# Two RMS norms moved onto scores and a last sum, and cross attention written as a pipeline of heads

## The chip, the cores and the metric

One Trainium2 chip, of which the kernel uses one core. The metric is the device time of one execution in microseconds (us), the median of several runs. The engines of the core are TensorE (PE, matmuls; PEld are its weight loads), VectorE (DVE), ScalarE (ACT), GpSimd (POOL) and SyncE (SP, which here issues the loads of weights). Each engine works through its own queue of instructions in order and waits at semaphores for the others.

## The reference

Two blocks of a language model on 256 tokens of 1024 features, all in float32: a first block (an RWKV mixer, an attention mixer, two gated feed-forward layers, layer norms) and a second one. The change touches the second half of the second block only:

```
def rmsnorm(x, g):
    y = xf * lax.rsqrt(jnp.mean(xf * xf, axis=-1, keepdims=True) + EPS)
    return y * g

def cross_attention(h, memn, w_q, w_kv, w_o):       # 4 heads of 256, 256 memory tokens
    q = (h @ w_q)
    k, v = jnp.split(memn @ w_kv, 2, axis=-1)
    s = jnp.einsum('bqhd,bmhd->bhqm', q, k) * (X_DH ** -0.5)
    p = jax.nn.softmax(s, axis=-1)
    o = jnp.einsum('bhqm,bmhd->bqhd', p, v)
    return o @ w_o

x = x + jnp.concatenate([ml_out, fx_out], axis=-1) @ w_out[l]
x = x + cross_attention(rmsnorm(x, ln_x[l]), rmsnorm(mem, ln_mem[l]), ...)
u = jax.nn.relu(rmsnorm(x, ln2[l]) @ w_ff1[l])
x = x + (u * u) @ w_ff2[l]
return rmsnorm(x, ln_f)
```

The factor of an RMS norm is one number per token. It can be taken out of a product with weights: the scores of a token scale with it, and so does relu, whose square scales with the factor squared.

## The kernel before

Tokens are two tiles of 128 (`t` = 0, 1), features eight tiles of 128 (`k` = 0 to 7). `x_tm` holds the residual with tokens on partitions, `ps` is PSUM with eight banks of 512 columns. A product in near-float32 takes three matmuls (`three`): every operand is split into a high part and the rest (`x_hi`, `x_lo`, `w_hi`, `w_lo`).

Weights come in slabs of 128x2048 in one fixed order: in the part in question `mix_o` (4 slabs), `x_q` (4), `x_o` (4), then `ff2` (32, up and down slabs in turn). SP loads slab i into one of three raw buffers (L531) as soon as `w_lo` of slab i-3 is written. ACT casts it to `w_hi` (`hi`, L575, from `after(i)` as slab i+3, which waits for `slab_done` of slab i), DVE writes `w_lo` (`lo`, L1248). PE waits for `lo_done` of a slab. All these stand at fixed places in the queues of ACT and DVE, between the work on activations. A "wide" slab is 48 matmuls of 256 columns (`wide_fm`), a "tall" slab is four units (`tall_unit`: token tile t, column half n) of six matmuls of 512 columns; a unit that ends a sum signals `bank_done` or `slab_done`.

`last_two(a, b, ...)` runs the last two slabs of a product in the order a(0,0) a(0,1) b(0,0) b(0,1) a(1,0) b(1,0) a(1,1) b(1,1). DVE adds each finished bank to `x_tm` (`add_product`, L1482). An RMS norm (`norm(6)` ahead of x_q, `norm(7)` ahead of ff2, `norm(8)` at the end) is then: ACT squares and sums the rows (L837, L846), takes the root (L838, L848), DVE the reciprocal (L1493), both write `xn` = x_tm * rstd (L1506, L862). PE transposes `xn` (L2289, 8 per token tile). ACT writes `x_hi` = transposed * gain for each k (L870), DVE `x_lo` (L1529). The first wide slab takes k by k as `x_lo` comes (`wide_as_ready`).

Cross attention is written stage by stage: four slabs of x_q with `xq_fm` taken by ACT (L978), the scores of all four heads (L2612), `masked` for all heads (DVE, row maximum, L1665), `exps` (ACT, L986), `probs` (DVE, L1678), transposes (L2362), `take_pt` (ACT, L993), outputs (L2621), `take_o` (ACT, two copies, L1001 and L1002; the next head's waits for `out_low` of this one) and `out_low` (DVE, L1683). `product("x_o", 12)` starts when all four heads are taken.

Of the kernel before, what the change touches and what calls it, by code (L numbers as in the profile page):

```python
# [13 lines left out]
P = 128  # L14
# [147 lines left out]
def build(nc, d, out, upto=99):  # L162
# [4 lines left out]
    with ExitStack() as ctx:  # L167
# [268 lines left out]
        rstd_ready, xn0_ready, xn_act, xn_dve = sem("rstd_ready"), sem("xn0_ready"), sem("xn_act"), sem("xn_dve")  # L436
        mem_loaded, final_ready = sem("mem_loaded"), sem("final_ready")
# [8 lines left out]
        STATS_BEFORE = {0: 0, 1: 2, 2: 4, 3: 6, 4: 8, 6: 11, 7: 14, 8: 17}  # L446
# [117 lines left out]
        def _(act):  # L564
# [330 lines left out]

            def norm(q, second=None):
# [7 lines left out]
                else:  # L904
# [4 lines left out]
                    if q == 8:  # L909
                        return  # L910
                    normalized(q, 1, x_tm)
# [232 lines left out]
            for i in range(2):  # L1144
                after(first["x_o"] + i)
            norm(7)
            for i in (2, 3):
                after(first["x_o"] + i)
            ffn("ff2")
# [86 lines left out]
        def _(dve):  # L1236
# [238 lines left out]
            def add_product(src, scale, t, n, last_slab, product, base=0):  # L1475
# [5 lines left out]
                at = src[:, t, 512 * n:512 * n + 512]  # L1481
                return V.scalar_tensor_tensor(at, at, scale, ps[:, base + 2 * t + n, :], ALU.mult, ALU.add)  # L1482
# [69 lines left out]
            def norm(q, scale, last_slab, product):  # L1552

                base = 0 if q else 2
                if NORMS[q][4]:
                    first_half_sums(scale, last_slab, product, base)
                    scales(q, 0)
                    link(add_product(x_tm, scale, 1, 1, last_slab, product, base))
                    link(half_statistics(1, 1))
                    mean_variance(1)  # L1560
                else:
                    add_product(x_tm, scale, 0, 0, last_slab, product)
                    add_product(x_tm, scale, 0, 1, last_slab, product).then_inc(stat_ready, 1)
                    add_product(x_tm, scale, 1, 0, last_slab, product).then_inc(stat_ready, 1)
                    scales(q, 0)
                    normalized(q, 0, slice(0, C), x_tm)
                    add_product(x_tm, scale, 1, 1, last_slab, product).then_inc(stat_ready, 1)
# [92 lines left out]
            def masked(u, s, tiles, mask):  # L1660
# [9 lines left out]
                V.tensor_scalar(mx[:, n:n + 2], rs[:, n:n + 2], -1.0, None, ALU.mult).then_inc(masked_ready, 1)  # L1670
# [218 lines left out]
            norm(6, 1.0, first["mix_o"] + 3, 5)  # L1889
            for i in (2, 3):  # L1890
                after(first["mix_o"] + i)
            for j in range(4):
                after(first["x_q"] + j)
            link(V.memset(zero_m[:, :], 0.0))
            for u in range(4):
                masked(U_X + u, cr_s, FULL, lambda w, t, c0, c1: zero_m[:, :])
            for u in range(4):
                probs(U_X + u, cr_s, FULL)
            for u in range(4):
                out_low(O_X + u, cr_o, slice(2 * u, 2 * u + 2))  # L1900
            for i in range(2):
                after(first["x_o"] + i)
            norm(7, 1.0, first["x_o"] + 3, 6)
            for i in (2, 3):
                after(first["x_o"] + i)
            ffn("ff2")
            last_norm(first["ff2"] + 31, 7)
# [3 lines left out]
        def _(pe):  # L1911
# [18 lines left out]
            def wide_as_ready(i, hi_x, lo_x, bank, order, x_ready):  # L1930
# [3 lines left out]
                for n, (k, count) in enumerate(order):  # L1934
                    pe.wait_ge(x_ready, count)
# [743 lines left out]
```

## Time and profile before

| | |
|---|---|
| runs | 1249.12, 1249.38 and 1252.03 us, median 1249.38 |
| profiled execution | 1249.55 us, of which the span is 1247.4 |
| DVE busy | 749.7 us, 60% |
| ACT busy | 596.4 us, 48% |
| POOL busy | 107.1 us, 9% |
| mean of the granted clock | 0.981 |
| DMA | 187.86 MB, mean 151 GB/s |

PE's row is in the rows below. The matmuls of the profile overlap (each is shown with its latency), so the spacing of their starts gives their cost, not their length: 0.23 us for 512 columns and 0.12 us for 256 at full clock. The span is what the instructions take; what lies around it is 2.15 us. The granted clock is a share of full speed: 1.00 is 2.4 GHz, 0.50 is 1.2 GHz.

### The profile page before, as it was taken

Reading aid. Unit: us, or ns where it says so; the run is one execution under the profiler, and the core shown is the slowest. Engines: PE = TensorE matmul, PEld = TensorE weight load, DVE = VectorE, ACT = ScalarE, POOL = GpSimd, SP = SyncE. Lnnn points to the kernel's source line nnn. Section 1 sums busy time; section 2 is a strip of 40 time slices with the busy share of each in tenths; the row PEclk is TensorE's granted clock in tenths of the full one; section 3 lists DMA queues with packets and bytes.
Section 4 is the critical chain, followed back from the end, with each engine's and each line's share of the span. In section 5 each row is a group of like instructions: output and inputs, shape, how many; then the busy total and the mean of one; then the engine's idle time right before and its main releaser. Section 6 shows DMA issues by size and latency. Waiting matters only on the chain.

```text
span 1247.4 us, 24447 instructions
## 1 busy us (share of the span) xinstructions
PE 1179.5 (95%) x10438; PEld 1054.7 (85%) x10438; DVE 749.7 (60%) x1078; ACT 596.4 (48%) x837; POOL 107.1 (9%) x87
## 2 busy tenths in 40 slices
PE   4999989989999999999999999799999998999997
PEld 4897777669999989877899999599988787999996
DVE  7888665364554466775555545767587553655554
ACT  4574543354434355554644344475555554544343
POOL 0032253501100000220010000000000000000000
PEclk9999999989999999999899999899999999999999
DMA  8431011046454545232455446335433342455550
GB/s 324 170 115 70 4 50 51 16 175 233 177 195 181 214 145 203 102 136 102 169 202 184 187 177 228 135 136 203 143 116 123 115 180 85 172 200 191 181 200 34
DMA packets 29417, 187.86 MB, mean 151 GB/s; under 512 B 3344, under 2 KB 5264, under 8 KB 8080
## 3 DMA queue, kind: packets, MB, share of 16 engines
q1 hardware_dynamic: 26544, 176.94, 38.6%
q10 hardware_dynamic: 2784, 9.60, 2.2%
q8 instruction: 71, 1.16, 0.4%
q14 instruction: 18, 0.15, 0.0%
HBM read 185.49 MB, written 1.05 MB: 150 GB/s over the span
## 4 chain that ended last, share of the span: by engine, by line
PE 83%; DVE 9%; ACT 5%; issue 2%; DMA 0%; POOL 0%; DVEq 0%; ACTq 0%; SPq 0%; POOLq 0%
PE ps L1914 24%; PE ps L1916 23%; PE ps L1915 23%; DVE w_lo L1248 2%; ACT w_hi L575 1%; PE ps L2032 1%; PE ps L2216 1%; ACT ma_s L986 1%; PE ps L2221 1%; PE ps L2218 1%; DVE mix_lo L1683 1%; DVE x_tm L1482 1%; PE ps L2362 1%; PE ps L2164 1%; PE ps L2612 1%
## 5 line engine op out<-in xcount | busy, mean ns | idle before, releaser
L1248 DVE TENSOR_TENSOR w_lo<-w_raw,w_hi 128x2048 fp32r<-128x2048 f32 x160 | 373.5, 2350 | 179.1 <-ACT w_hi L575 178.5
L1914 PE MATMUL ps<-x_hi,w_hi 128*128 128x256 f32 x1344 | 382.9, 285 | 4.2 <-DVE x_lo L1520 2.2
L575 ACT CAST w_hi<-w_raw 128x2048 fp32r<-128x2048 f32 x158 | 300.7, 1906 | 177.8 <-PE ps L1916 174.4
L1915 PE MATMUL ps<-x_lo,w_hi 128*128 128x256 f32 x1344 | 379.3, 282 | 0.0
L1916 PE MATMUL ps<-x_hi,w_lo 128*128 128x256 f32 x1344 | 379.2, 282 | 0.0
L1914 PEld LDWEIGHTS ps<-x_hi,w_hi 128*128 128x128 f32 x1344 | 257.2, 191 | 11.3 <-issue 9.5
L1915 PEld LDWEIGHTS ps<-x_lo,w_hi 128*128 128x128 f32 x1344 | 257.1, 191 | 2.2 <-issue 0.7
L1916 PEld LDWEIGHTS ps<-x_hi,w_lo 128*128 128x128 f32 x1344 | 257.0, 191 | 0.0
L1914 PE MATMUL ps<-w_hi,hid_hi 128*128 128x512 f32 x304 | 119.8, 394 | 0.1
L1916 PE MATMUL ps<-w_hi,hid_lo 128*128 128x512 f32 x304 | 119.4, 393 | 0.0
L1915 PE MATMUL ps<-w_lo,hid_hi 128*128 128x512 f32 x304 | 118.4, 390 | 0.0
L1638 DVE TENSOR_TENSOR hid<-act_f,ps 128x512 f32<-128x512 f32 x22 | 15.1, 688 | 130.3 <-PE ps L1916 130.3
L950 ACT ACTIVATE act_f<-ps 128x512 f32<-128x512 f32 x38 | 22.8, 599 | 131.1 <-PE ps L1916 131.1
L1914 PE MATMUL ps<-w_hi,mix_hi 128*128 128x512 f32 (+1 forms) x192 | 73.4, 382 | 4.7 <-DVE mix_lo L1348 2.7
L1916 PE MATMUL ps<-w_hi,mix_lo 128*128 128x512 f32 (+1 forms) x192 | 68.5, 357 | 0.0
L1915 PE MATMUL ps<-w_lo,mix_hi 128*128 128x512 f32 (+1 forms) x192 | 68.4, 356 | 0.0
L1916 PEld LDWEIGHTS ps<-w_hi,hid_lo 128*128 128x128 f32 x304 | 57.1, 188 | 13.2
L1915 PEld LDWEIGHTS ps<-w_lo,hid_hi 128*128 128x128 f32 x304 | 57.1, 188 | 11.3
L1914 PEld LDWEIGHTS ps<-w_hi,hid_hi 128*128 128x128 f32 x304 | 57.1, 188 | 11.1 <-DVE hid_lo L1644 0.5
L1914 PE MATMUL ps<-w_hi,x_hi 128*128 128x256 f32 x224 | 65.0, 290 | 0.0
L1915 PE MATMUL ps<-w_lo,x_hi 128*128 128x256 f32 x224 | 62.9, 281 | 0.0
L1916 PE MATMUL ps<-w_hi,x_lo 128*128 128x256 f32 x224 | 62.9, 281 | 0.0
(367 smaller groups left out, 1716.8 us busy)
## 6 DMA issues: line engine op xcount, KB each, us to landing
w_raw<-in_weights SPq DMA_DIRECT2D x164, 1024.0 KB, 4.8
xt<-in_xT SPq DMA_DIRECT2D x2, 512.0 KB, 5.7
x_tm<-in_x SPq DMA_DIRECT2D x1, 1024.0 KB, 4.8
gain<-in_mix_g ACTq DMA_DIRECT2D x2, 512.0 KB, 4.6
gain<-in_mix_b ACTq DMA_DIRECT2D x2, 512.0 KB, 5.6
gain<-in_ffn_g ACTq DMA_DIRECT2D x2, 512.0 KB, 7.1
gain<-in_ffn_b ACTq DMA_DIRECT2D x2, 512.0 KB, 8.8
gain<-in_mem ACTq DMA_DIRECT2D x1, 1024.0 KB, 4.8
```

What stands on the lines that cost most here:

```text
L575: nc.scalar.copy(w_hi[:, i % WS, :], w_raw[:, i % RAW, :]).then_inc(hi_done, 1)
L950: nc.scalar.activation(act_f[:, j % 2, :], ps[:, 4 + 2 * (j % 2), :], ACT.Relu if name == "ff2" else ACT.Silu).then_inc(ffn_act, 1)
L986: ins = nc.scalar.activation(s[:, u % 4, c0:c1], s[:, u % 4, c0:c1], ACT.Exp, bias=mx[:, 2 * (u % 4) + t:2 * (u % 4) + t + 1], accum_out=s ...
L1248: V.tensor_tensor(w_lo[:, i % WS, :], w_raw[:, i % RAW, :], w_hi[:, i % WS, :].bitcast(F32), ALU.subtract).then_inc(lo_done, 1)
L1482: return V.scalar_tensor_tensor(at, at, scale, ps[:, base + 2 * t + n, :], ALU.mult, ALU.add)
L1638: V.tensor_tensor(hid[:, j % 2, :], act_f[:, j % 2, :], ps[:, 5 + 2 * (j % 2), :], ALU.mult).then_inc(ffn_taken, 1)
L1683: V.tensor_tensor(mix_lo[:, f2, :], o_sb[:, :, :], mix_hi[:, f2, :].bitcast(F32), ALU.subtract).then_inc(o_lo_done, 1)
L1914: nc.tensor.matmul(out, hi_l, hi_r, start=start, stop=False)
L1915: nc.tensor.matmul(out, hi_l, lo_r, start=False, stop=False)
L1916: return nc.tensor.matmul(out, lo_l, hi_r, start=False, stop=stop)
L2032: last = mm(both[q][:, T * m:T * m + T], src[f, 2 * m + t, :], ar[f, 2 * g + m, t, :, :].rearrange("p s c -> p (s c)"), start=True, stop=True)
L2164: last = mm(ps[0:hi_c - lo_c, 5, at:at + T], g1[:, k, lo_c:hi_c], mixed[:, 1, k, :], start=k == 0, stop=k == KT - 1)
```

## The change

1. Norms 6 and 7 no longer write `xn` ahead of the product. PE transposes the unscaled `x_tm`: 12 of the 16 transposes stand inside `last_two`, between a(1,1) and b(1,1); the last four, which need the last sum, stand inside the first wide slab, behind its first two k.
2. The squares and roots run later, in `late_squares`, on ACT behind the casts that follow `x_hi`. For norm 6 the factor is applied in `exps` (as the scale) and in `masked` (to the row maximum). For norm 7 it is the factor squared (`ACT.Identity` in place of `ACT.Sqrt`) and is applied when the sum of ff2 is added to `x_tm`.
3. DVE does the sums in `sums_and_features`, with `x_lo` of the first two k ahead of the last sum.
4. Cross attention is a pipeline: projections, scores, softmax, transposes, outputs and the first half of x_o are interleaved by head, on PE, ACT and DVE. Outputs go to banks 4 to 7 instead of 0 to 3.

```diff
+            def late_squares(q):
+                e, n = NORMS[q][3], FM_NORMS.index(q)
+                for t in range(TT):
+                    act.wait_ge(xn_act if t else xn0_ready, n + 1)
+                    link(nc.scalar.activation(xn[:, t, :], x_tm[:, t, :], ACT.Square, accum_out=square[:, t:t + 1]))
+                    nc.scalar.activation(sd[:, t:t + 1], square[:, t:t + 1], ACT.Identity if q == 7 else ACT.Sqrt,
+                                         scale=1.0 / C, bias=eps_c[:, e:e + 1]).then_inc(sd_ready, 1)
...
-            norm(6)
+            features(6)
             for i in (2, 3):
                 after(first["mix_o"] + i)
-            takes("x_q", 4, lambda j: xq_fm[:, 2 * j:2 * j + 2, :], lambda j: (C // 4) ** -0.5)
-            for u in range(4):
-                exps(U_X + u, cr_s, FULL)
-            for u in range(4):
-                take_pt(U_X + u, cr_p, 512)
-            for u in range(4):
-                take_o(O_X + u, u, cr_o, slice(2 * u, 2 * u + 2))
+            late_squares(6)
...
+            take_xq(0)
+            take_xq(1)
+            exps(U_X, cr_s, FULL)
+            take_xq(2)
+            exps(U_X + 1, cr_s, FULL)
+            take_pt(U_X, cr_p, 512)
+            take_xq(3)
+            take_xo(0)
+            take_pt(U_X + 1, cr_p, 512)
+            exps(U_X + 2, cr_s, FULL)
+            exps(U_X + 3, cr_s, FULL)
+            take_xo(1)
+            after(first["x_o"])
+            take_pt(U_X + 2, cr_p, 512)
+            take_pt(U_X + 3, cr_p, 512)
+            take_xo(2)
+            take_xo(3)
+            after(first["x_o"] + 1)
...
-            norm(7)
+            features(7)
             for i in (2, 3):
                 after(first["x_o"] + i)
+            late_squares(7)
             ffn("ff2")
...
+            def sums_and_features(q, last_slab, product):
+                add_product(x_tm, 1.0, 0, 0, last_slab, product)
+                add_product(x_tm, 1.0, 0, 1, last_slab, product).then_inc(xn0_ready, 1)
+                add_product(x_tm, 1.0, 1, 0, last_slab, product).then_inc(xn_dve, 1)
+                features(q, range(2))
+                add_product(x_tm, 1.0, 1, 1, last_slab, product).then_inc(xn_act, 1)
+                features(q, range(2, KT))
...
+                if product == 7:
+                    return V.scalar_tensor_tensor(at, ps[:, base + 2 * t + n, :], rstd[:, t:t + 1], at, ALU.mult, ALU.add)
...
+            after(first["x_q"])
+            after(first["x_q"] + 1)
+            masked(U_X, cr_s, FULL, no_mask)
+            probs(U_X, cr_s, FULL)
+            after(first["x_q"] + 2)
+            masked(U_X + 1, cr_s, FULL, no_mask)
+            probs(U_X + 1, cr_s, FULL)
+            after(first["x_q"] + 3)
+            out_cross(0)
+            masked(U_X + 2, cr_s, FULL, no_mask)
+            masked(U_X + 3, cr_s, FULL, no_mask)
+            probs(U_X + 2, cr_s, FULL)
+            probs(U_X + 3, cr_s, FULL)
+            out_cross(1)
+            after(first["x_o"])
+            out_cross(2)
+            out_cross(3)
...
                 for n, (k, count) in enumerate(order):
+                    if late and n == 2:
+                        transposed(late, 1, range(4, KT))
...
                     tall_unit(a, hi_a, lo_a, False, False, 1, n)
+                    if q and n:
+                        transposed(q, 0, range(KT))
+                        transposed(q, 1, range(4))
                     tall_unit(b, hi_b, lo_b, False, True, 1, n)
...
+            cross_project(0)
+            cross_project(1)
+            cross_scores(0)
+            cross_project(2)
+            cross_scores(1)
+            p_transposes(U_X, cr_s, "full")
+            cross_project(3)
+            cross_outputs(0)
+            p_transposes(U_X + 1, cr_s, "full")
+            cross_scores(2)
+            cross_scores(3)
+            cross_outputs(1)
+            pe.wait_ge(o_lo_done, O_X + 1)
+            wait_slab(pe, first["x_o"])
+            for t in range(TT):
+                for n in range(2):
+                    cross_unit(0, t, n)
+            p_transposes(U_X + 2, cr_s, "full")
+            p_transposes(U_X + 3, cr_s, "full")
+            pe.wait_ge(o_lo_done, O_X + 2)
+            wait_slab(pe, first["x_o"] + 1)
+            cross_unit(1, 0, 0)
+            cross_unit(1, 0, 1)
+            cross_outputs(2)
+            cross_outputs(3)
+            cross_unit(1, 1, 0)
+            cross_unit(1, 1, 1)
+            pe.wait_ge(o_lo_done, O_X + 3)
+            last_two(first["x_o"] + 2, first["x_o"] + 3, ..., (o_lo_done, O_X + 4), 7)
```

What stood on PE between the end of the product `mix_o` and the first slab of x_q before (`base_c` is the identity matrix, the first row is the last of b(1,1)):

```order
L1916 MATMUL ps<-w_hi,mix_lo 128x512
L2289 MATMUL ps<-base_c,xn 128x128 [waits xn0_ready]
L2289 MATMUL ps<-base_c,xn 128x128 x7
L2289 MATMUL ps<-base_c,xn 128x128 [waits xn_dve]
L2289 MATMUL ps<-base_c,xn 128x128 x3
L2289 MATMUL ps<-base_c,xn 128x128 [waits xn_act]
L2289 MATMUL ps<-base_c,xn 128x128 x3
L1914 MATMUL ps<-x_hi,w_hi 128x256 [waits xlo_ready,lo_done,p_taken]
```

And at the same place now, from the last matmul of a(1,1) into b(1,1):

```order
L1968 MATMUL ps<-w_hi,mix_lo 128x512
L2342 MATMUL ps<-base_c,x_tm 128x128 [waits xn0_ready]
L2342 MATMUL ps<-base_c,x_tm 128x128 x7
L2342 MATMUL ps<-base_c,x_tm 128x128 [waits xn_dve]
L2342 MATMUL ps<-base_c,x_tm 128x128 x3
L1966 MATMUL ps<-w_hi,mix_hi 128x512
L1967 MATMUL ps<-w_lo,mix_hi 128x512
```

The transposes read `x_tm` and moved ahead of the last unit; the other four stand twelve matmuls into the first slab of x_q.

What stood on ACT behind the product before (`raw_loaded2` is the cast of the second slab of x_q, `raw_loaded0` that of the third):

```order
L837 ACTIVATE xn,square<-x_tm 128x1024 [waits stat_ready]
L838 ACT_TABLE_LOAD
L838 ACTIVATE sd<-square,eps_c 128x1 [waits act_step]
L846 ACTIVATE xn,square<-x_tm 128x512 [waits stat_ready]
L851 ACTIVATE square<-square,eps_c 128x1 [waits act_step]
L846 ACTIVATE xn,square<-x_tm 128x512 [waits stat_ready,act_step]
L848 ACTIVATE sd<-square 128x1 [waits act_step]
L862 ACTIVATE xn<-x_tm,rstd 128x512 [waits rstd_ready]
L870 ACTIVATE x_hi<-ps,par 128x256 [waits tr_ready] x8
L575 CAST w_hi<-w_raw 128x2048 [waits slab_done,raw_loaded2]
L575 CAST w_hi<-w_raw 128x2048 [waits slab_done,raw_loaded0]
L978 ACTIVATE xq_fm<-ps 128x512 [waits slab_done]
```

And now:

```order
L871 ACTIVATE x_hi<-ps,par 128x256 [waits tr_ready] x8
L576 CAST w_hi<-w_raw 128x2048 [waits slab_done,raw_loaded2]
L576 CAST w_hi<-w_raw 128x2048 [waits slab_done,raw_loaded0]
L902 ACTIVATE xn,square<-x_tm 128x1024 [waits xn0_ready]
L903 ACT_TABLE_LOAD
L903 ACTIVATE sd<-square,eps_c 128x1 [waits act_step]
L902 ACTIVATE xn,square<-x_tm 128x1024 [waits xn_act]
L903 ACTIVATE sd<-square,eps_c 128x1 [waits act_step]
L986 ACTIVATE xq_fm<-ps 128x512 [waits slab_done]
```

The squares moved behind `x_hi` and two casts, the normalised halves are gone. Ahead of ff2 the same rows stand in the same order, without the table load, and the next row is `act_f` of the first step. On DVE the softmax of a head now stands between the slabs of weights:

```order
L1273 TENSOR_TENSOR w_lo<-w_raw,w_hi 128x2048 [waits hi_done]
L1693 ISA cr_s,rs<-ps,zero_m 128x256 [waits scores_ready]
L1693 ISA rs 128x1
L1693 ISA cr_s,rs<-ps,zero_m 128x256
L1693 ISA rs 128x1
L1700 SCALAR_TENSOR_TENSOR mx<-rs,rstd 128x2 [waits rstd_ready,dve_step]
L1709 RECIPROCAL rs<-sm 128x2 [waits exp_ready]
L1711 TENSOR_SCALAR cr_s<-cr_s,rs 128x256 [waits dve_step]
L1711 TENSOR_SCALAR cr_s<-cr_s,rs 128x256
L1273 TENSOR_TENSOR w_lo<-w_raw,w_hi 128x2048 [waits hi_done]
```

This is head 0, with `w_lo` of the first x_o slab ahead of it and of the second behind; before, all six `w_lo` stood ahead of the softmax of all heads.

## Rows read from the trace of the kernel before

**Rows 1.** The page, part 1: busy us, share of the span, instructions.

```profile
PE 1179.5 (95%) x10438; PEld 1054.7 (85%) x10438; DVE 749.7 (60%) x1078; ACT 596.4 (48%) x837; POOL 107.1 (9%) x87
```

**Rows 2.** Windows: length, busy us (count) of PE, PEld, DVE, ACT, POOL; clock; DMA; GB/s.

```profile
989.00:992.00 3.00, 3.00 (x14) 3.00 (x15) 2.56 (x7) 3.00 (x6) 0.00 (x0) 0.51 0.00 0
...
1021.30:1023.00 1.70, 0.00 (x0) 0.00 (x1) 1.63 (x9) 1.70 (x9) 0.00 (x0) 1.00 0.44 183
```

**Rows 3.** Timeline at norm 6: start, length, instruction, [idle before, releaser].

```profile
982.82 0.39 PE L1914 MATMUL ps<-w_hi,mix_hi 128*128 128x512 f32 x1
...
984.19 1.03 PE L2289 MATMUL ps<-base_c,xn 128*128 128x128 f32 x8
...
984.38 0.69 DVE L1482 SCALAR_TENSOR_TENSOR x_tm<-x_tm,ps 128x512 f32<-128x512 f32 x1 [0.98 <-PE ps L1916]
...
986.99 1.09 PE L2289 MATMUL ps<-base_c,xn 128*128 128x128 f32 x8 [1.77 <-DVE xn L1506]
...
987.46 3.03 ACT L870 ACTIVATE x_hi<-ps,par 128x256 fp32r<-128x256 f32 x8 [0.29 <-PE ps L2289]
...
988.96 0.46 PE L1914 MATMUL ps<-x_hi,w_hi 128*128 128x256 f32 x1 [0.89 <-DVE x_lo L1529]
```

**Rows 4.** Timeline of ACT and DVE, slabs q0 to q2.

```profile
990.33 3.76 ACT L575 CAST w_hi<-w_raw 128x2048 fp32r<-128x2048 f32 x2
...
992.31 4.50 DVE L1248 TENSOR_TENSOR w_lo<-w_raw,w_hi 128x2048 fp32r<-128x2048 f32 x2 [0.75 <-ACT w_hi L575]
...
996.42 0.60 ACT L978 ACTIVATE xq_fm<-ps 128x512 f32<-128x512 f32 x1 [2.33 <-PE ps L1916]
...
1002.08 0.60 ACT L978 ACTIVATE xq_fm<-ps 128x512 f32<-128x512 f32 x1 [3.27 <-PE ps L1916]
```

**Rows 5.** Groups of instructions from 1013 to 1035: count, busy us, mean ns.

```profile
L2612 PE MATMUL ps<-xk_fm,xq_fm 128*128 128x256 f32 x32 | 7.2, 382 | 0.7 <-ACT xq_fm L978 0.7
...
L2621 PE MATMUL ps<-cr_p,gain 128*128 128x256 f32 x32 | 7.1, 379 | 0.0
```

**Rows 6.** Timeline in cross attention.

```profile
1018.40 0.42 DVE L1665 CUSTOM_DVE_ANT_0 cr_s<-ps,zero_m 128x256 f32<-128x256 f32 x1
...
1019.41 0.51 ACT L986 ACTIVATE cr_s<-cr_s,mx 128x256 f32<-128x256 f32 x1 [2.35 <-DVE mx L1670]
...
1023.00 0.42 PEld L2362 LDWEIGHTS ps<-base_c,cr_s 128*128 128x128 f32 x4 [2.19 <-DVE cr_s L1678]
```

**Rows 7.** Timeline at norm 7 and the first steps of ff2.

```profile
1051.76 1.06 ACT L837 ACTIVATE xn<-x_tm 128x1024 f32<-128x1024 f32 x1 [4.20 <-DVE x_tm L1482]
...
1052.93 1.28 ACT L838 ACT_TABLE_LOAD   x1
...
1054.23 0.29 ACT L838 ACTIVATE sd<-square,eps_c 128x1 f32<-128x1 f32 x1
...
1054.92 0.39 PE L1914 MATMUL ps<-w_hi,mix_hi 128*128 128x512 f32 x1
...
1068.35 0.60 ACT L950 ACTIVATE act_f<-ps 128x512 f32<-128x512 f32 x1 [2.16 <-PE ps L1916]
...
1073.74 0.47 PE L1914 MATMUL ps<-w_hi,hid_hi 128*128 128x512 f32 x1
```

**Rows 8.** Timeline at the last norm.

```profile
1237.49 0.30 ACT L838 ACTIVATE sd<-square,eps_c 128x1 f32<-128x1 f32 x1
...
1239.20 1.28 DVE L1605 SCALAR_TENSOR_TENSOR xn<-x_tm,rstd,gain 128x1024 f32<-128x1024 f32 x1
...
1241.08 0.69 DVE L1482 SCALAR_TENSOR_TENSOR x_tm<-x_tm,ps 128x512 f32<-128x512 f32 x1 [0.59 <-PE ps L1916]
```

**Rows 9.** Timeline and window (columns as in rows 2) around another fall of the clock.

```profile
268.01 1.16 PE L2289 MATMUL ps<-base_c,xn 128*128 128x128 f32 x8 [2.62 <-ACT xn L859]
...
274.00:276.00 2.00, 2.00 (x12) 2.00 (x12) 1.88 (x5) 1.75 (x4) 0.00 (x0) 0.58 0.00 0
```

**Rows 10.** The page, part 6: DMA issues, KB each, median us to landing.

```profile
w_raw<-in_weights SPq DMA_DIRECT2D x164, 1024.0 KB, 4.8
```

More of the change, by code:

```diff
@@ L908, in norm @@
                         squares_of_half(q, n)
[L909 to L911 removed]
+                    return
                 features(q)
@@ L1554, in norm @@
                 base = 0 if q else 2
[L1555 to L1567, printed above, removed]
+                first_half_sums(scale, last_slab, product, base)
+                scales(q, 0)
+                link(add_product(x_tm, scale, 1, 1, last_slab, product, base))
+                link(half_statistics(1, 1))
+                mean_variance(1)
                 scales(q, 1)
@@ L1887, in _, with out_cross @@
             after(first["mix_o"] + 1)
-            norm(6, 1.0, first["mix_o"] + 3, 5)
+            sums_and_features(6, first["mix_o"] + 3, 5)
             for i in (2, 3):
                 after(first["mix_o"] + i)
[L1892 to L1899, printed above, removed]
-                out_low(O_X + u, cr_o, slice(2 * u, 2 * u + 2))
-            for i in range(2):
-                after(first["x_o"] + i)
-            norm(7, 1.0, first["x_o"] + 3, 6)
+            for t in range(TT):
+                scales(6, t)
+            V.memset(zero_m[:, :], 0.0).then_inc(zero_set, 1)
+            dve.wait_ge(zero_set, 1)
+            no_mask = lambda w, t, c0, c1: zero_m[:, :]
+            def out_cross(u):
+                out_low(O_X + u, cr_o, slice(2 * u, 2 * u + 2))
+            after(first["x_q"])
[15 more added lines that the diff above has]
+            out_cross(3)
+            after(first["x_o"] + 1)
+            sums_and_features(7, first["x_o"] + 3, 6)
             for i in (2, 3):
@@ L1906, in _ @@
             ffn("ff2")
+            for t in range(TT):
+                scales(7, t)
+            dve.wait_ge(rstd_ready, 16)
             last_norm(first["ff2"] + 31, 7)
@@ L2347, in ffn, with project @@
                     step(j)
-            def project(n, i, wide, order=None):
+            def project(n, i, wide, order=None, late=None):
                 if n >= 3:
@@ L2353, in project @@
                 if order:
-                    wide_as_ready(i, x_hi, x_lo, n % 3, order, xlo_ready)
+                    wide_as_ready(i, x_hi, x_lo, n % 3, order, xlo_ready, late)
                 else:
@@ L2602, in _, with cross_project, cross_scores @@
             last_two(first["mix_o"] + 2, first["mix_o"] + 3, mix_hi[:, 4:6, :], mix_lo[:, 4:6, :], mix_hi[:, 6:8, :],
[L2603 to L2609 removed]
+                     mix_lo[:, 6:8, :], (o_lo_done, O_FX + 4), 6)
+            def cross_project(j):
+                project(P_FIRST["x_q"] + j, first["x_q"] + j, wide_fm, None if j else k_order(6),
+                        None if j else 6)
+            def cross_scores(u):
+                pe.wait_ge(p_taken, P_FIRST["x_q"] + u + 1)
                 for t in range(TT):
@@ L2614, in _, with cross_outputs @@
                 last.then_inc(scores_ready, 1)
-            for u in range(4):
-                p_transposes(U_X + u, cr_s, "full")
-            for u in range(4):
+            def cross_outputs(u):
                 pe.wait_ge(pt_taken, U_X + u + 1)
@@ L2620, in _, with cross_unit @@
                     for tk in range(TT):
-                        last = mm(ps[:, u, T * m:T * m + T], gain[:, tk, T * u + P * m:T * u + P * m + P],
+                        last = mm(ps[:, 4 + u, T * m:T * m + T], gain[:, tk, T * u + P * m:T * u + P * m + P],
                                   cr_p[:, u, T * tk:T * tk + T], start=tk == 0, stop=tk == 1)
                 last.then_inc(o_ready, 1)
-            product("x_o", 12)
-            transposes(7)
+            def cross_unit(i, t, n):
+                tall_unit(first["x_o"] + i, mix_hi[:, 2 * i:2 * i + 2, :], mix_lo[:, 2 * i:2 * i + 2, :], i == 0, i == 3, t, n)
+            cross_project(0)
[12 more added lines that the diff above has]
+            wait_slab(pe, first["x_o"])
+            for t in range(TT):
+                for n in range(2):
[11 more added lines that the diff above has]
+            pe.wait_ge(o_lo_done, O_X + 3)
+            last_two(first["x_o"] + 2, first["x_o"] + 3, mix_hi[:, 4:6, :], mix_lo[:, 4:6, :], mix_hi[:, 6:8, :],
+                     mix_lo[:, 6:8, :], (o_lo_done, O_X + 4), 7)
             ffn("ff2", 7)
```

69 lines of the change are left out of this document (32 added, 37 removed).

## Prediction

> **What bounds the kernel now.** I read the page's busy times first: TensorE (PE) is busy 95% of the span [rows 1], so what a change can take away is PE's own work or one of its few idle places. Then the granted clock by windows, for what an idle place costs afterwards [rows 2], and then the timeline around the three places that the change touches, which shows who ends each wait. Names: the slabs of weights are q0 to q3 (x_q), o0 to o3 (x_o), f0, f1, ... (ff2); units are six 512-column matmuls; a and b are the last two slabs of a product. All times are of the profiled execution, 1249.55 us with a span of 1247.4; the median of the runs is 1249.38, 0.17 lower.
>
> Norm 6 [rows 3]: the last unit of the product, b(1,1), issues from 982.82 to 984.19. The projection starts at 988.96. Between them PE runs only two groups of 8 transposes (1.03 and 1.09 us); the rest is the chain sum, squares, root, factor, normalised half, transposes, x_hi, x_lo. Then the clock is 0.51 between 989 and 992 [rows 2], the lower level (1.2 GHz). So q0, 48 matmuls, ends only at about 996.07 (ACT takes it at 996.42, 0.35 after PE's last issue, [rows 4]). At full clock a wide slab takes 5.66 (996.42 to 1002.08). Norm 7 repeats this 72.10 later.
>
> Cross attention [rows 5, 6]: q3 ends near 1013.0, x_o starts at 1034.4 (1054.92 [rows 7], the end of its unit a(1,1), less 15 units at 1.365). These 21.4 us hold 7.2 of scores, about 1.7 of transposes and 7.1 of outputs; the rest, about 5.4, is waiting: for the softmax (PE is at 0.00 between 1021.3 and 1023, [rows 2]), the last xq_fm, and the copies of heads 1 to 3 one after another.
>
> **Norm 6, new order.** Transposes of x_tm: 12 stand in front of b(1,1), four behind k=0 and k=1 of q0. Each takes 0.129 (1.03/8). They start where b(1,1) did, at 982.82: the sums that they read are those of the units up to b(1,0), which were through a unit earlier. b(1,1) runs 984.37 to 985.74. ACT starts x_hi 0.47 behind the transposes of its pair (986.99 to 987.46), so at 984.32, and PE can use the first k 1.50 after that (988.96), x_lo in between: at 985.8, as it comes free. The four late transposes need the last sum, which starts 0.19 after the end of b(1,1)'s issues (984.19 to 984.38) and takes 0.69: written at 986.6 to 986.7, for DVE has x_lo of two k ahead of it, in time for PE at 987.2. x_hi of k=4 is then at 987.67, and each further k comes every 0.38 (3.03/8) against PE's 0.71 per k. No wait, no fall of the clock: q0 ends at 985.8 + 5.66 + 0.52 = 992.0, 4.1 earlier.
>
> A wait takes its place. The cast of q1 stands behind all eight x_hi on ACT, and starts at 989.1; w_lo of q1 starts 1.98 later and takes 2.29 [rows 4]: ready at 993.4. PE waits 1.4 us, q1 ends at 999.07 instead of 1001.72. **Norm 6 is worth 2.65.** Behind it the squares of late_squares run while PE is in q1 and hold xq_fm of head 0 back to 997.9, before scores(0) at 999.1.
>
> **Cross attention, new order.** PE's work from 999.07 to the end of a(1,1) of x_o: scores 7.18, q2 and q3 11.32, transposes 16 x 0.105 = 1.68 (0.42 for four, [rows 6]), outputs 7.07, and 15 of 16 units at 1.365 (six issues, 982.82 to 984.19, [rows 3]) = 20.5: 47.75. If nothing is late, a(1,1) ends at 1046.8; before, the same point is 1054.92 [rows 7].
>
> What could be late is the softmax, since casts and w_lo of slabs stand in its queues. Head 0: o0's w_lo ends at 1004.4, masked and mx take 1.0 (1018.40 to 1019.41, [rows 6]), two exps 1.0, probs 0.9: 1007.4, PE comes at 1008.35. Outputs(0) is the narrow place: q2 ends 1006.5, ACT takes it at 1006.9, cast of o1 at 1007.4, w_lo 1009.35 to 1011.6, masked(1) 1012.6, exps(1) 1013.65, copy of P(0) 1014.35; PE has filled the time with scores(1), transposes(0) and q3 and arrives at 1014.4: no margin. Outputs(1): copy at 1019.0, PE at 1020.3. x_o's first unit: mix_lo of head 0 at 1020.2, PE at 1022.1. Outputs(2): ACT waits in after(o0) for o0's slab to end (1027.5), casts 1.9, copies P(2): 1030.5, PE at 1031.1. Second half of x_o: mix_lo of head 2 at 1034.9, of head 3 at 1036.9, needed at 1037.4 and 1040.1. I add 0.3 for handovers that miss by tenths. The bounds of this sum: none late, 0; each of outputs(0), (1), (2) 1.5 later than worked out, 1.5 + 0.2 + 0.9 = 2.6. Loads have to keep up: a load lands 4.8 after its issue [rows 10]; o0's is issued when w_lo of q1 ends, 993.4, lands near 998.2 and is cast at 1000.3.
>
> **Norm 7.** Up to f0 the same: a(1,1) at 1046.8, 12 transposes, b(1,1) to 1049.8, f0 from 1049.9 to 1056.1; f1's cast starts at 1053.2, its w_lo is ready at 1057.5, PE waits 1.4, f1 ends at 1063.15. But here late_squares stands in front of act_f(0). Square, accumulator and root take 1.18 when the table load of 1.28 is taken out (1051.76 to 1054.23, [rows 7]), with the root's own 0.25 1.42, twice 2.84: from 1056.95 to 1059.8. act_f(0) was 5.39 ahead of the first down slab (1068.35 to 1073.74, [rows 7]): hid, cast of f3, hid_hi, w_lo, hid_lo. So PE starts that slab at 1065.15, after a second wait of 2.0. Before it was 1073.74: **8.6 earlier**, of which norm 7 gives 0.6 on top of the 8.0 so far. The gap of norm 7 is not removed, it is exchanged for waits of 1.4 and 2.0. Behind it hid(1), f3 and f4 are ready before PE asks.
>
> **The end.** In the changed order Sqrt is no longer the last table before norm 8, so a load of 1.28 stands in front of the root of t=0. It delays that root from 1237.49 to 1238.8, and result(0), 1.28 long and 1.7 behind the root's start now because the third sum is ahead of it, to about 1240.6; the last sum starts at 1241.08 [rows 8]. Hidden by 0.5; without that cover it would cost 1.28. The product's factor changes the operands of add_product, not its kind, its reciprocals stand behind the last hid_lo, and final_g's load only moves behind the cast of f0, 200 us ahead of its use: 0. The trace has no wait between a table load and the activation after it (load 1052.93 + 1.28, root at 1054.23). The Trainium skill (ScalarE: Activation LUTs, What ACT_TABLE_LOAD costs) puts about 1.38 us of drain on top of the load's 1.28. By that rule result(0) would end at 1242.0 and the last sum would be 0.9 later, and the time that much higher; the trace does not show the drain, so I stay with 0.
>
> **Sum.** 2.65 + 5.4 + 0.6 = 8.6, less 0.3: 8.3. 1249.55 - 8.3 = 1241.2.
>
> **Rivals.**
> A, the clock falls in the new waits. Single idle stretches of 1.7 (1021.3 to 1023) left it at 1.00, and the gap of norm 6, 1.77 and 0.89 idle with transposes between, lowered it. After 2.62 idle at 268.01 it fell too, and was still at 0.58 between 274 and 276 [rows 2, 9]. The new 2.0 lies between. If it falls there as after norm 6 (0.51 over 3 us, 1.5 lost), 1242.7; in both norms, up to 1244.2.
> B, the heads starve. outputs(0) to (2) miss as bounded above, or a load lands late: 2.6 to 4 lost, 1244 to 1245.5. For it: no margin at outputs(0). Against: every other margin is 0.6 to 17.
> C, the full gain: the new waits don't come, because q1, f1 and act_f(0) are ready. 1.4 + 1.4 + 2.0 more, 1236.4. Against: the order of ACT's queue.
> D, slower: the clock. After 268.01 it stayed low up to 276 [rows 9], at most 4.0 lost (half of 8). Were that so at four places (q1, outputs(0), f1, f0's hid), the loss is 16, the time 1257; from three places on the kernel is slower than now. Against: dense matmuls on both sides of each place.
> E, a change without effect: PE waits elsewhere by as much. That gives 1249. The order shows no such place behind the first down slab of ff2.
>
> **Numbers.** Forecast 0.52, A 0.20, B 0.15, C 0.07, D 0.03, E 0.03. The predicted time is the forecast's, 1241.2. The range goes from 1238.0 (the waits shorter by half and more) to 1246.0 (B whole). 0.3% is 3.7 us, about what the runs can tell from no change: faster than 1245.6 hold the forecast, A, C and most of B, 0.88; same 0.09; slower 0.03.
>
> **What would show it.** In the changed profile: transposes of x_tm between two units at full clock; PEclk 1.00 where q0 and f0 run; PE waiting for w_lo at q1 and f1, about 1.4 each, and for hid_lo ahead of the first down slab, about 2.0; none above 0.5 between the scores of head 0 and x_o. Wrong would be: q0 waiting for x_lo, a wait of a microsecond for a copy of P, a cast waiting for its load, or the last sum later relative to the end.

## The result, and the profile after the change

| | median us | lowest to highest | runs |
|---|---|---|---|
| before, same chip | 1247.61 | 1245.29 to 1252.03 | 6 |
| changed kernel | 1238.97 | 1236.38 to 1240.22 | 6 |
| predicted | 1241.2 | 1238.0 to 1246.0 | |

The ratio is 0.993, with a 95% interval of 0.9912 to 0.9947: faster by 8.6 us, with 6.6 to 11 from the interval. Forecast were 8.3. The time itself was forecast 2.2 too high, and 1.9 of that is the base: the forecast started from the profiled 1249.55, and the median before is 1247.61. The profiled execution took 1239.38 us, with a span of 1236.3 at a mean clock of 0.987; before it was 1249.55, 1247.4 and 0.981. So the two profiles differ by 11.1 us of span, more than the medians. The first task is to split these 11.1.

Busy times on the page, in the columns of [rows 1]:

```profile
PE 1174.0 (95%) x10438; PEld 1049.8 (85%) x10438; DVE 747.3 (60%) x1074; ACT 593.7 (48%) x829; POOL 107.1 (9%) x87
```

The number of matmuls is the same. PE's busy time is 5.5 us less, though no instruction was taken from it: the mean granted clock was 0.987 instead of 0.981. How much of the 5.5 that makes was not worked out.

PE's waits in the changed kernel from 970 us to the end (waited for: us in total, times, longest):

```profile
PE ps L1966 <- DVE w_lo L1273: 2.7, 2, 1.4
PE ps L1966 <- DVE hid_lo L1672: 1.5, 1, 1.5
```

The kernel before, from 1000 us on, so without norm 6:

```profile
PE ps L2362 <- DVE cr_s L1678: 1.8, 1, 1.8
PE ps L2289 <- DVE xn L1506: 1.8, 1, 1.8
PE ps L1914 <- ACT mix_hi L1002: 1.6, 1, 1.6
PE ps L1914 <- DVE x_lo L1529: 0.9, 1, 0.9
PE ps L2612 <- ACT xq_fm L978: 0.7, 1, 0.7
```

All the old waits are gone, those of cross attention too, and exactly the three new ones that were forecast are there. PE's timeline of the changed kernel shows where (start, length, instruction, [idle before, releaser]):

```profile
981.17 1.47 PE L2342 MATMUL ps<-base_c,x_tm 128*128 128x128 f32 x12
982.39 0.48 PE L1966 MATMUL ps<-w_hi,mix_hi 128*128 128x512 f32 x1
...
983.96 0.36 PE L1966 MATMUL ps<-x_hi,w_hi 128*128 128x256 f32 x1
...
985.45 0.60 PE L2342 MATMUL ps<-base_c,x_tm 128*128 128x128 f32 x4
...
991.70 0.36 PE L1966 MATMUL ps<-x_hi,w_hi 128*128 128x256 f32 x1 [1.32 <-DVE w_lo L1273]
...
997.43 1.89 PE L2662 MATMUL ps<-xk_fm,xq_fm 128*128 128x256 f32 x8
...
1012.53 1.89 PE L2670 MATMUL ps<-cr_p,gain 128*128 128x256 f32 x8
...
1044.69 1.47 PE L2342 MATMUL ps<-base_c,x_tm 128*128 128x128 f32 x12
...
1055.23 0.35 PE L1966 MATMUL ps<-x_hi,w_hi 128*128 128x256 f32 x1 [1.36 <-DVE w_lo L1273]
...
1062.56 0.50 PE L1966 MATMUL ps<-w_hi,hid_hi 128*128 128x512 f32 x1 [1.49 <-DVE hid_lo L1672]
...
1229.47 0.40 PE L1968 MATMUL ps<-w_hi,hid_lo 128*128 128x512 f32 x1
```

Read from the top: 12 transposes behind a(1,1), then b(1,1), then q0 without a wait (before there was a gap of 1.77 and one of 0.89, [rows 3]); four more transposes inside q0; then q1 late by 1.32. The scores of head 0 at 997.43 mark the end of q1. The outputs of head 0 show no wait. At norm 7 the same pattern comes again, and the first down slab is late by 1.49.

The clock at these places, by windows (columns as in [rows 2], clock behind the last bracket):

```profile
983.00:992.00 9.00, 7.68 (x59) 7.06 (x58) 6.66 (x11) 7.16 (x11) 0.00 (x0) 1.00 0.00 0
...
1060.00:1066.00 6.00, 4.51 (x25) 3.73 (x24) 5.57 (x5) 3.01 (x4) 0.00 (x0) 1.00 0.79 299
```

1.00 in both, where it was 0.51 behind norm 6 [rows 2].

**Three stretches.** To compare profiles I cut the end of the program at four points that every kernel has: the end of a(1,1) of mix_o (before: 982.82, [rows 3]; now 981.17), the end of a(1,1) of x_o (1054.92, [rows 7]; now 1044.69), the start of the first down slab of ff2 (1073.74, [rows 7]; now 1062.56), and PE's last matmul (1229.47 here; in the kernel before, next row).

```profile
1240.64 0.40 PE L1916 MATMUL ps<-w_hi,hid_lo 128*128 128x512 f32 x1
```

A is norm 6 and cross attention, B is norm 7 and the first two slabs of ff2, C the rest. In kernels with the old order, where the transposes stand behind b(1,1), its 1.365 is taken off to find the end of a(1,1). "Fall" says whether the clock fell behind norm 6 / norm 7. All in us, one profile each ("wait": it fell behind the new wait ahead of the first down slab):

```
kernel             A      B      C       A+B+C    fall
before             72.10  18.82  166.90  257.82   yes/yes
before_third       70.77  17.67  166.80  255.25   no/no
changed            63.52  17.87  166.91  248.30   no/no
changed_again      63.47  17.89  166.92  248.28   no/no
norms_only         69.19  17.86  166.92  253.97   no/no
pipeline_only      66.15  17.63  166.82  250.60   yes/no
norm7_old          63.49  17.62  166.82  247.92   no/no
squares_later      63.49  16.22  166.80  246.51   no/no
both_moves         62.50  15.31  166.81  244.62   no/no
squares_twice      63.48  20.23  169.48  253.19   no/wait
```

So of the 11.1 us between the two profiles 8.6 came in A and 0.95 in B. Another 1.65 (982.82 less 981.17) lie ahead of the change, in code that both kernels share. They are not the change's doing. Behind PE's last matmul 6.83 are left of the span (1236.3 less 1229.47), and before it was 6.76 (1247.4 less 1240.64).

### The profile page after: what moved, and what is told of

The parts are those of the page before. It is cut to its first block, busy times and chain, and to the rows that moved or that the text cites. A ratio compares the mean times of both kernels' runs of the same rounds, so it can differ in the third digit from the quotient of the medians.

```text
span 1236.3 us, 24438 instructions
## 1 busy us (share of the span) xinstructions
PE 1174.0 (95%) x10438; PEld 1049.8 (85%) x10438; DVE 747.3 (60%) x1074; ACT 593.7 (48%) x829; POOL 107.1 (9%) x87
## 3 DMA queue, kind: packets, MB, share of 16 engines
q8 instruction: 71, 1.16, 0.4%
## 4 chain that ended last, share of the span: by engine, by line
PE 83%; DVE 9%; ACT 5%; issue 2%; DMA 0%; POOL 0%; ACTq 0%; DVEq 0%; SPq 0%; POOLq 0%
PE ps L1966 24%; PE ps L1968 23%; PE ps L1967 22%; DVE w_lo L1273 3%; ACT w_hi L576 2%; PE ps L2086 1%; PE ps L2270 1%; PE ps L2342 1%; ACT ma_s L994 1%; PE ps L2411 1%; PE ps L2275 1%; PE ps L2272 1%; PE ps L2218 1%; PE ps L2662 1%; PE ps L2670 1%
## 5 line engine op out<-in xcount | busy, mean ns | idle before, releaser
L1966 PEld LDWEIGHTS ps<-x_hi,w_hi 128*128 128x128 f32 x1344 | 254.1, 189 | 14.4 <-issue 11.3
L1967 PEld LDWEIGHTS ps<-x_lo,w_hi 128*128 128x128 f32 x1344 | 254.1, 189 | 2.3 <-issue 0.7
L1968 PEld LDWEIGHTS ps<-x_hi,w_lo 128*128 128x128 f32 x1344 | 254.1, 189 | 0.0
```

The source lines that it names most:

```text
L1966: nc.tensor.matmul(out, hi_l, hi_r, start=start, stop=False)
L1967: nc.tensor.matmul(out, hi_l, lo_r, start=False, stop=False)
L1968: return nc.tensor.matmul(out, lo_l, hi_r, start=False, stop=stop)
```

## The experiments

Theory: norm 6 gives 2.65 by removing gap and fall, the pipeline some 5.4, norm 7 exchanges its gap for two waits and gives little. Rivals: the pipeline gives nearly all; or the gain is mostly the clock.

**One half at a time.** norms_only keeps the new norms and puts cross attention back in stages; pipeline_only keeps the old norms and has the pipeline.

```diff
 norms_only (PE; ACT and DVE likewise; both against the changed kernel)
-            cross_project(0)
-            cross_project(1)
-            cross_scores(0)
...
+            for j in range(4):
+                project(P_FIRST["x_q"] + j, first["x_q"] + j, wide_fm, None if j else k_order(6), None if j else 6)
+            pe.wait_ge(p_taken, P_FIRST["x_q"] + 4)
+            for u in range(4):
                 for t in range(TT):
                     for k in range(2):
...
 pipeline_only (ACT)
-            features(6)
+            norm(6)
...
-            features(7)
+            norm(7)
```

> Both norms as in the changed kernel, cross attention stage by stage as before. My theory (each norm exchanges its gap for a wait for w_lo, norm 7 for a second one behind the late squares): 2.7 us from norm 6 and 0.8 from norm 7, 3.5 faster than the kernel before. PE waits for w_lo at q1 and f1, 1.3 each, and 1.5 for hid_lo; the waits of the softmax (1.8, 1.6, 0.7) are all there. Rival (the norms give their whole gaps, the pipeline little): 4.1 each, 8 us faster.

> The kernel before with cross attention as the pipeline of heads, both norms old. My theory: 5.4 to 6.0 us faster than the kernel before, with no wait of PE above 0.5 between the scores of head 0 and x_o, and both gaps at the norms (1.8 and 0.9, the clock at 0.51 behind them). The parts add up: this and norms_only together are the change's 8.7 to 9.5. Rival (whole gaps of the norms): 1 us faster. Rival (the heads starve without the time that norm 6 gave): a wait for a copy of P at outputs(0) of 1 us or more, 3 to 4 faster.

norms_only: 1242.54 us (7 runs), ratio 0.9952 (0.9938 to 0.9967). pipeline_only: 1238.99 (6 runs), ratio 0.9934 (0.9913 to 0.9955). Before, on the same chip: 1248.74. The medians do not resolve the parts: two halves of 6.2 and 9.8 us would make 16, and the 4.1 us at which the interval of norms_only begins is above the 3.85 by which its A+B+C is shorter than the kernel before's. Where the rest comes from is open; code ahead of the change varies by more from one execution to the next (last section).

The stretches do resolve them. norms_only has the waits that were expected, 1.34 and 1.35 for w_lo, 1.50 for hid_lo and the three of cross attention; its A is 2.91 and its B 0.96 shorter than in the kernel before, where 2.7 and 0.8 were expected. pipeline_only has the same fall behind norm 6 as the kernel before, and its A is 72.10 - 66.15 = 5.95 shorter. That is the pipeline's worth. (In A+B+C the two halves make 3.85 + 7.22 = 11.07 instead of 9.52, mostly because the fall behind norm 7 is missing in both and so is counted twice.) Replacing then norm 6 (norm7_old below) takes A from 66.15 to 63.49: 2.66, forecast 2.65. PE's waits in pipeline_only from 970 us to the end:

```profile
PE ps L2319 <- DVE xn L1522: 3.5, 2, 1.8
PE ps L1944 <- DVE x_lo L1545: 1.8, 2, 0.9
```

These are the two old norms' gaps alone: no head waits for anything, so the rival that the heads starve is refuted here too.

**The new norm 7 taken back.**

```diff
-            features(7)
+            norm(7)
             for i in (2, 3):
                 after(first["x_o"] + i)
-            late_squares(7)
```

(and `transposes(7)` back behind the product, no factor in ff2's sum.)

> The changed kernel with norm 7 as before (squares, root and normalised rows ahead of the transposes). My theory: only 0.8 us slower than the changed kernel, since norm 7's gap of 4.1 went into waits of 1.4 and 1.5 and 0.4 of delayed starts. Rival (the gap is gained whole): 4 us slower than the changed kernel.

The time was 1236.39 (6 runs), ratio 0.9897 (0.988 to 0.9913). The expectation failed: the old norm 7 is not slower. B is 17.62 against 17.87 of the changed kernel, and A+B+C is 0.4 shorter. The rows show why, in norm7_old at norm 7:

```profile
1055.12 1.09 PE L2346 MATMUL ps<-base_c,xn 128*128 128x128 f32 x8 [1.77 <-DVE xn L1532]
1057.10 0.36 PE L1970 MATMUL ps<-x_hi,w_hi 128*128 128x256 f32 x1 [0.89 <-DVE x_lo L1555]
1068.57 0.39 PE L1970 MATMUL ps<-w_hi,hid_hi 128*128 128x512 f32 x1
```

The waits are the old ones, 1.77 and 0.89. But from 1057.10 to 1068.57 there are 11.47 us for f0 and f1, full speed: the clock did not fall. Before it had (0.50 between 1062 and 1064, in the windows of the kernel before further down). The forecast had priced norm 7 with that fall.

**Squares moved, doubled, and casts moved.** These test the two new waits. squares_later moves norm 7's squares behind the first steps of ff2:

```diff
                 for j in range(FFN_PEEL):
                     step(j)
+                if name == "ff2":
+                    late_squares(7)
...
-            late_squares(7)
             ffn("ff2")
```

> The changed kernel with late_squares(7) on ACT behind the third step of ff2 instead of ahead of its first. If the squares ahead of act_f(0) are what PE waits for at the first down slab (1.5 us for hid_lo): that wait is gone or under 0.1, 1.4 to 1.5 us faster than the changed kernel. Rival (the wait of f1 for w_lo sets hid as well, or another wait takes its place): under 0.5 faster.

1237.43 us (5 runs), ratio 0.9911 (0.9897 to 0.9924). The wait for `hid_lo` is gone; of PE's waits from 970 us on one line is left:

```profile
PE ps L1967 <- DVE w_lo L1274: 2.7, 2, 1.4
```

B is 16.22, so 1.65 shorter, and A+B+C is 1.79 shorter than the changed kernel's (expected: 1.4 to 1.5). The medians of this kernel and the changed one, 1.5 apart and from two chips, are too close to tell them apart.

squares_twice does the squares of norm 7 once more ahead of `late_squares(7)`:

```diff
+            act.wait_ge(xn0_ready, FM_NORMS.index(7) + 1)
+            act.wait_ge(xn_act, FM_NORMS.index(7) + 1)
+            for t in range(TT):
+                link(nc.scalar.activation(xn[:, t, :], x_tm[:, t, :], ACT.Square, accum_out=square[:, t:t + 1]))
             late_squares(7)
```

> The changed kernel with both squares of norm 7 done twice ahead of act_f(0). Every microsecond of ACT there is PE's: two squares and accumulators are 2.3 us more, so PE's wait for hid_lo goes from 1.5 to 3.8. If the clock falls in a wait that long, 1.5 us come on top and PEclk is at 0.5 behind it. Rival (another engine sets the first down slab): the wait grows by less than 1.

1242.81 us (9 runs), ratio 0.9954 (0.9938 to 0.997). ACT in squares_twice, the passes ahead of `act_f`:

```profile
1056.78 1.07 ACT L1176 ACTIVATE xn<-x_tm 128x1024 f32<-128x1024 f32 x1
1057.73 0.20 ACT L1176 ACTIVATION_READ_ACCUMULATOR xn<-x_tm 128x1 f32 x1
...
1059.15 1.07 ACT L902 ACTIVATE xn<-x_tm 128x1024 f32<-128x1024 f32 x1
...
1061.91 0.58 ACT L958 ACTIVATE act_f<-ps 128x512 f32<-128x512 f32 x1
```

and PE with the windows around it:

```profile
1067.26 0.80 PE L1970 MATMUL ps<-w_hi,hid_hi 128*128 128x512 f32 x1 [3.81 <-DVE hid_lo L1676]
```

```profile
1066.00:1070.00 4.00, 2.74 (x7) 2.16 (x8) 4.00 (x5) 1.70 (x2) 0.00 (x0) 0.50 0.53 195
1070.00:1072.00 2.00, 2.00 (x6) 1.61 (x5) 0.61 (x2) 0.00 (x0) 0.00 (x0) 0.50 0.74 250
1072.00:1074.00 2.00, 2.00 (x8) 1.60 (x8) 0.00 (x0) 0.00 (x0) 0.00 (x0) 0.80 0.91 381
```

2.37 us more of squares (1056.78 to 1059.15) become 2.32 more of wait (3.81 for 1.49): every microsecond of ACT ahead of `act_f` goes straight to PE. Here the clock did fall: it is 0.50 from 1066 on, so it fell inside the wait, before PE went on at 1067.26, and C is 2.6 longer (expected were 1.5).

both_moves has squares_later and also casts the next slab between the two halves of `x_hi`, at both norms:

```diff
                     for k in range(KT):
+                        if k == 4:
+                            after(first["mix_o" if q == 6 else "x_o"] + 2)
                         to_features(q, k).then_inc(xhi_ready, 1)
...
             features(6)
-            for i in (2, 3):
-                after(first["mix_o"] + i)
+            after(first["mix_o"] + 3)
```

> squares_later, and the cast of q1 and of f1 on ACT between x_hi of k=3 and k=4, where ACT has 1.8 us to spare for the last four transposes. If the place of the cast in ACT's queue makes PE wait at q1 and f1: w_lo starts right behind x_lo of k=7 instead of 0.9 later, the waits go from 1.35 to 0.5 or 0.6, 1.5 us faster than squares_later from norm 6 to the end. Rival (DVE is the one behind, w_lo would be no earlier): both waits stay at 1.3. Rival (the casts delay x_hi of k=4): a new wait for x_lo of up to 0.3 in q0 and f0.

1235.07 us (6 runs), ratio 0.9888 (0.9863 to 0.9913): 12.9 below the median of the kernel before on the same chip (1248.01), and the lowest median here, though the kernels ran on different chips. ACT in both_moves:

```profile
982.98 1.57 ACT L871 ACTIVATE x_hi<-ps,par 128x256 fp32r<-128x256 f32 x4 [8.65 <-PE ps L2343]
984.42 1.92 ACT L576 CAST w_hi<-w_raw 128x2048 fp32r<-128x2048 f32 x1
986.38 1.57 ACT L871 ACTIVATE x_hi<-ps,par 128x256 fp32r<-128x256 f32 x4
```

and its PE waits from 970 us on:

```profile
PE ps L1967 <- DVE w_lo L1274: 0.8, 2, 0.4
```

In the changed kernel ACT is idle between the halves, waiting for the last four transposes:

```profile
985.87 1.57 ACT L871 ACTIVATE x_hi<-ps,par 128x256 fp32r<-128x256 f32 x4 [1.84 <-PE ps L2342]
```

A cast of 1.92 takes the place of these 1.84, and the second half starts no later for it: 4.69 behind the start of the 12 transposes, where it was 4.70. The waits of 1.32 and 1.36 shrink to 0.37 and 0.40, and A+B+C is 1.89 shorter than that of squares_later. Both are a little better than expected (waits of 0.5 to 0.6, 1.5 shorter), and no wait for x_lo came.

**Does the order decide whether the clock falls?** Pipeline_only and norm7_old kept the gap of norm 7 and showed no fall, the kernel before had one. That could be the order of work or chance. So three of the kernels were profiled again, and the changed one too.

> The kernel before, profiled once more. Open is whether the fall of the clock behind norm 7 belongs to the gap: it fell there in the first profile (0.51 over 3 us), and did not in those of pipeline_only and norm7_old, whose gap is the same. If it belongs to the kernel's order: low behind both norms again, 257.8 us from the end of a(1,1) of mix_o to PE's last matmul. If it depends on the moment at which the gap comes: high behind one norm or both, and 1.4 us less for each.

> norm7_old, profiled once more: high clock behind norm 7 again and 247.9 us over the same stretch, if the moment of the gap within this kernel decides; low and 249.3 us, if it is chance.

> The kernel before, a third profile. So far the clock fell behind norm 7 in 2 of 2 profiles of this kernel and in 0 of 3 of the kernels with the pipeline in front of the same old gap. If the order in front of the gap decides: low again behind norm 7, 257.8 us from the end of a(1,1) of mix_o to PE's last matmul. If it is chance with even odds: as likely high, 256.4.

> pipeline_only, profiled once more. If the order decides: low behind norm 6, high behind norm 7, 250.6 us over that stretch again. If it is chance: as likely low behind norm 7, and 252.0.

> norm7_old, a third profile. If the order decides: high behind norm 7, 247.9 us. If it is chance: as likely low, and 249.3.

> The changed kernel, profiled once more. Its waits are set by the queues of ACT and DVE and not by the clock: 1.3, 1.4 and 1.5 again at q1, f1 and the first down slab, no fall of the clock behind the norms, 248.3 us over the stretch.

Times, one run each: before_again 1246.26, norm7_old_again 1234.96, before_third 1245.85, pipeline_only_again 1240.62, norm7_old_third 1237.97, changed_again 1239.09. The repeats agree in A+B+C with their first profile to 0.1 (before_again 257.83, pipeline_only_again 250.58, norm7_old_again 247.98, norm7_old_third 247.96, changed_again 248.28), with one exception: before_third, at 255.25. Around norm 7 in the kernel before:

```profile
1060.00:1062.00 2.00, 1.11 (x6) 0.97 (x5) 1.57 (x4) 2.00 (x7) 0.00 (x0) 0.68 0.00 0
1062.00:1064.00 2.00, 2.00 (x12) 2.00 (x11) 1.66 (x5) 2.00 (x3) 0.00 (x0) 0.50 0.00 0
```

and in before_third, the same program:

```profile
1057.00:1059.00 2.00, 1.11 (x10) 0.91 (x9) 1.44 (x4) 2.00 (x7) 0.00 (x0) 1.00 0.00 0
1059.00:1061.00 2.00, 2.00 (x20) 2.00 (x19) 1.78 (x5) 2.00 (x3) 0.00 (x0) 1.00 0.00 0
```

Its gap of norm 7 is the same:

```profile
1056.21 1.09 PE L2289 MATMUL ps<-base_c,xn 128*128 128x128 f32 x8 [1.77 <-DVE xn L1506]
1058.19 0.36 PE L1914 MATMUL ps<-x_hi,w_hi 128*128 128x256 f32 x1 [0.89 <-DVE x_lo L1529]
```

Same program, same gap to 0.01 us, and the clock falls or doesn't. Over all profiles the gap of 1.77 and 0.89 was followed by a fall behind norm 6 in 4 of 5 (two of three of the kernel before, both of pipeline_only), behind norm 7 in 2 of 8 (two of three of the kernel before, none of the five with the pipeline). A single fall costs 1.33 in A (72.10 less 70.77) and 1.15 in B (18.82 less 17.67); by before_again, with 71.93 and 18.96, it is 1.16 and 1.29. "The order decides" is refuted as a rule, since before_third breaks it. What does decide is open; 5 of 5 with the pipeline may still be more than chance.

## Why the prediction was right, step by step

- **Transposes inside the product, q0 without a wait: right.** The frame of the changed profile is 1.65 earlier. q0 starts at 983.96 (forecast 985.8 - 1.65 = 984.15), q1 at 991.70 (993.4 - 1.65 = 991.75) and ends at 997.43 (999.07 - 1.65 = 997.42).
- **Norm 6 worth 2.65: right against the profile read, too large as a mean.** From the end of a(1,1) to that of q1 it was 18.90 and is 16.26: 2.64. Half of it is the fall. Against before_third A gives 70.77 - 69.19 = 1.6 for it (norms_only), and 1.3 when the pipeline's 5.95 is taken from the 7.25 between before_third and the changed kernel.
- **Cross attention 5.4 less 0.3: direction and place right, the term was mis-sized.** It gave 5.95, twice (53.19 to 47.26 in the changed kernel; pipeline_only). The 0.3 for missed handovers did not occur. The rest is in the scores and outputs, which I had priced at the busy times of their groups, 7.18 and 7.07. Between other work they take 6.72 and 6.53 from start to start: outputs(0) holds PE from 1012.53 until 1014.26, 1.73 for eight. The units came out at 20.94, not 20.5, which gives 0.4 of that back. The three idle places of cross attention in the first fence of waits make only 4.1 (0.7, 1.8, 1.6), so waits alone would have been too small a price; which rows hold the other 1.8 was not broken down. The narrow place was seen rightly: the copy of P(0) ends 0.19 ahead of PE in the row of ACT that follows.

```profile
1011.78 0.56 ACT L1001 COPY cr_p<-ps 128x512 f32<-128x512 f32 x1
```

- **Norm 7 worth 0.6: mis-sized, and by its sign unsafe.** In the profile pair it is 0.95 (18.82 to 17.87). The forecast wait of 2.0 was 1.49, because late_squares begins 9.74 behind the end of a(1,1) (1054.43 less 1044.69) and not 10.15; the rest of its chain went as worked out, 2.78 to `act_f` (forecast 2.84) and 5.35 from there to the slab (5.39). But 1.15 of the gain is the fall that went. Without it the new norm 7 loses 0.25 in B (17.87 against 17.62). The measured worth lies between -0.4 (A+B+C of norm7_old, where C is 0.1 shorter too) and +0.95. That it "is not removed, it is exchanged" was right.
- **The end at no cost: right.** C differs by 0.01, but C ends at PE's last matmul; behind that the changed kernel takes 0.07 more (6.83 to 6.76). The last sum starts 0.43 behind PE's last matmul, as before (0.44, [rows 8]), and takes 0.75 instead of 0.69: changed operands, which the forecast put at nothing, cost 0.06. The added table load in the changed kernel, and what it was to be hidden by:

```profile
1226.36 1.28 ACT L839 ACT_TABLE_LOAD   x1
...
1227.66 0.29 ACT L839 ACTIVATE sd<-square,eps_c 128x1 f32<-128x1 f32 x1
...
1228.25 1.28 DVE L1633 SCALAR_TENSOR_TENSOR xn<-x_tm,rstd,gain 128x1024 f32<-128x1024 f32 x1
...
1229.90 0.75 DVE L1508 SCALAR_TENSOR_TENSOR x_tm<-ps,rstd,x_tm 128x512 f32<-128x512 f32 x1 [0.37 <-PE ps L1968]
```

  DVE is idle for 0.37 between result(0) and the last sum (forecast 0.5). The root starts 0.02 behind the load's end. The Trainium skill (ScalarE: Activation LUTs, What ACT_TABLE_LOAD costs) adds a drain of about 1.38 us to a load. This trace does not show it: the root follows at once.
- **Rival A, a fall in the new waits: did not come** in any of the 16 single waits of 1.3 to 1.5 us at q1, f1 and the first down slab. With 3.81 (squares_twice) it came. A wait of 1.42 elsewhere was followed by a fall too (last section), so that none came here is not explained. **B and C**: no head starved, and the waits did come. C's idea was sound, though: both_moves takes 3.7 of its 4.8 by moving two things on ACT.

That the sum came out near the measured 8.6 is partly luck: without any fall A+B+C gives 255.25 - 248.30 = 6.95, with both falls 9.5. The median lies between, as it would if the clock fell in some executions of the kernel before and not in others; the executions without a profile do not show it. The forecast of 8.3 read one profile with both falls and was low by 0.8 in the pipeline.

## What to carry to other kernels

Where PE is busy 95% of the time, what a reordering can win is the list of its idle places plus the fall of the clock behind them; price the two apart, for the fall may come in one execution and not in the next. When a chain of waiting is taken out of PE's path, look at what its work now stands in front of in ACT's queue (here casts and `act_f`): each microsecond ahead of `act_f` was a microsecond of PE. Compare profiles over stretches with fixed marks, not by their spans.

## What was not expected of the hardware

- **The granted clock is not a function of the program alone.** Besides the norms, the clock can fall behind a wait of 1.42 ahead of the product with `gst`, in code that all kernels share. In the changed kernel (949.08, idle 1.42 before) it fell there:

```profile
950.00:952.00 2.00, 2.00 (x13) 2.00 (x13) 1.90 (x8) 0.00 (x0) 0.00 (x0) 0.61 0.95 393
952.00:954.00 2.00, 2.00 (x12) 2.00 (x11) 1.90 (x16) 1.74 (x8) 0.00 (x0) 0.54 0.01 4
```

  In the kernel before, with the same wait of 1.42 ahead of 952.05, it did not:

```profile
953.00:957.00 4.00, 4.00 (x36) 4.00 (x35) 3.79 (x22) 1.76 (x8) 0.00 (x0) 1.00 0.43 176
```

  This wait stands in all 14 profiles, at 1.41 to 1.43, and the clock fell behind it in 8: not in the first profile of the kernel before but in both repeats, in both profiles of the changed kernel, in the first of norm7_old and not in its repeats. Here the same program and the same wait gave both outcomes again.

  The Trainium skill (TensorE: Matmul & The Clock Gate, What's actually happening) says that the window in which the array's activity is watched is free-running, "it doesn't reset when your kernel starts". By that rule the same gap may fall differently to it from one execution to the next, which would be the chance seen here. No run here shows that window, so that this is the cause was not shown.

  So what the prediction read, that a single idle stretch of 1.7 leaves the clock alone, holds for the one seen there and not in general. Behind the 16 single waits of 1.3 to 1.5 at q1, f1 and the first down slab no fall came, behind this one 8 of 14. The work around it is different: ahead of it stand 16 matmuls with 64 rows and 128 columns (from 945.33 on in the changed kernel), not ones of 128 rows. Whether that is the reason was not tested.
- **Identical code ahead of the change varies by 9.2 us.** The end of a(1,1) of mix_o came at 987.47 in norm7_old and at 978.25 in norm7_old_again, the same program. Between 100 and 300 us the first has a clock of 0.92:

```profile
100.00:300.00 200.00, 185.66 (x3402) 151.32 (x3402) 116.90 (x230) 87.44 (x198) 62.81 (x55) 0.92 0.22 77
```

  and the second 0.98:

```profile
100.00:300.00 200.00, 184.89 (x3444) 151.21 (x3441) 122.77 (x233) 90.93 (x198) 65.51 (x57) 0.98 0.24 86
```

  This spread is larger than the whole effect of the change, and it is why the halves could not be told by spans or by a few times.
